# Query parts, weight splits and PSUM banks before the first attention, rearranged

## What is computed

```python
hn = rms_norm(h, kv_norm_g)              # normalised with one gain
v  = hn @ w_v                            # "att_v": units 88 to 95
k  = hn @ w_k                            # "att_kq": even units 96, 98, ...
q  = rms_norm(h, g[0]) @ w_q             # "att_kq": odd units 97, 99, ...
...                                      # scores per head pair, masked softmax, values, then w_o
h = h + rms_norm(m, g[1])
```

## Time and profile before

| what | us |
|---|---|
| median of 3 runs | 2521.54 |
| lowest and highest of them | 2517.85, 2522.76 |
| the profiled execution's own time | 2520.23 |
| its span | 2518.4 |
| TensorE busy in it | 2399.2 |
| VectorE, ScalarE, GpSimd busy | 1370.1, 783.0, 446.5 |

### The profile page before, as it was taken

How to read it: one execution, slowest core, us unless ns; L and a number is a source line. 1 busy time by engine, 2 the same in 40 slices (tenths; PEclk the granted TensorE clock), 3 DMA queues, 4 the chain that set the end, 5 groups by cost and what they waited for, 6 DMA issues and landing times.

```text
span 2518.4 us, 28995 instructions
## 1 busy us (share of the span) xinstructions
PE 2399.2 (95%) x10924; PEld 1934.3 (77%) x10924; DVE 1370.1 (54%) x1951; ACT 783.0 (31%) x1242; POOL 446.5 (18%) x203
## 2 busy tenths in 40 slices
PE   6789999997999899999999999998999999999997
PEld 5677888876766788888788888766877888888886
DVE  5666444446467644434555435789664454444465
ACT  2114323222233333223332223341244343222233
POOL 6670000003545200000000000456540000000000
PEclk8899999997999999999999999999999999999999
DMA  4232433321222233333143332223211343333221
GB/s 169 68 91 67 117 99 94 96 71 50 83 81 84 67 105 96 93 98 102 53 118 100 99 89 81 74 67 93 67 55 55 100 127 91 109 94 99 86 78 54
DMA packets 64833, 221.94 MB, mean 88 GB/s; under 512 B 7504, under 2 KB 9680, under 8 KB 64592
## 3 DMA queue, kind: packets, MB, share of 16 engines
q1 hardware_dynamic: 59184, 208.17, 27.9%
q10 hardware_dynamic: 5536, 12.19, 1.5%
HBM read 218.23 MB, written 2.10 MB: 87 GB/s over the span
## 4 chain that ended last, share of the span: by engine, by line
PE 83%; DVE 11%; ACT 3%; issue 2%; DMA 0%; POOL 0%; ACTq 0%; DVEq 0%; POOLq 0%
PE PS L435 23%; PE PS L437 22%; PE PS L436 22%; PE PS L454 3%; PE PS L531 2%; PE PS L458 1%; DVE SS L1344 1%; DVE MK L1705 1%; PE PS L681 1%; DVE SC L1680 1%; PE PS L505 1%; PE PS L702 1%; PE PS L691 1%; DVE TOP L1704 1%; PE PS L827 1%
## 5 line engine op out<-in xcount | busy, mean ns | idle before, releaser
L435 PE MATMUL PS<-XH,WH 128*128 128x512 f32 x1632 | 647.2, 397 | 19.6 <-DVE T L1542 12.5
L437 PE MATMUL PS<-XH,WL 128*128 128x512 f32 x1632 | 637.0, 390 | 0.0
L436 PE MATMUL PS<-XL,WH 128*128 128x512 f32 x1632 | 636.6, 390 | 0.0
L1332 DVE TENSOR_TENSOR WL<-RAW,WH 128x1024 fp32r<-128x1024 f32 (+3 forms) x308 | 362.2, 1176 | 224.3 <-ACT WH L977 219.7
L378 POOL TENSOR_TENSOR WH<-RAW,ONES 128x1024 fp32r<-128x1024 f32 x91 | 182.7, 2008 | 1437.3 <-DVE WL L1332 735.9
L977 ACT ACTIVATE WH<-RAW 128x1024 fp32r<-128x1024 f32 (+3 forms) x312 | 315.2, 1011 | 354.6 <-DVE M L1449 202.4
L435 PEld LDWEIGHTS PS<-XH,WH 128*128 128x128 f32 x1632 | 307.2, 188 | 101.3 <-issue 22.8
L435 PE MATMUL PS<-HH,WH 128*128 128x512 f32 x928 | 364.1, 392 | 2.6 <-DVE HL L1418 2.6
L437 PE MATMUL PS<-HH,WL 128*128 128x512 f32 x928 | 361.4, 389 | 0.0
L436 PE MATMUL PS<-HL,WH 128*128 128x512 f32 x928 | 361.2, 389 | 0.0
L437 PEld LDWEIGHTS PS<-XH,WL 128*128 128x128 f32 x1632 | 307.1, 188 | 65.1
(11 more groups left out here) (237 smaller groups left out, 2732.8 us busy)
## 6 DMA issues: line engine op xcount, KB each, us to landing
RAW<-in_weights SPq DMA_DIRECT2D x379, 512.0 KB, 3.5
RAW<-in_weights SPq DMA_DIRECT2D x16, 384.0 KB, 3.1
H<-in_xT ACTq DMA_DIRECT2D x8, 256.0 KB, 8.4
BIAS<-in_rel ACTq DMA_DIRECT2D x8, 256.0 KB, 3.5
RAW<-in_weights SPq DMA_DIRECT2D x8, 256.0 KB, 2.6
out<-R ACTq DMA_DIRECT2D x8, 256.0 KB, 2.2
BIAS<-in_rel ACTq DMA_DIRECT2D x8, 224.0 KB, 3.9
DECAY<-in_decay ACTq DMA_DIRECT2D x1, 1024.0 KB, 4.9
```

Source lines behind the costliest of these rows:

```text
L435: nc.tensor.matmul(PS[:, bank_, :], high[:, w], xh[:, k, :], start=(k == 0), stop=False)
L436: nc.tensor.matmul(PS[:, bank_, :], high[:, w], xl[:, k, :], start=False, stop=False)
L437: return nc.tensor.matmul(PS[:, bank_, :], low[:, w], xh[:, k, :], start=False, stop=stop)
L1332: V.tensor_tensor(low[:, 0:w], RAW[:, slot, 0:w], high[:, 0:w].bitcast(F32), ALU.subtract).then_inc(weights_split, 1)
```

## The change

1. `POOL_RANGES` and `WIDE`: units 92 to 99 are no longer split by GpSimd, which goes on at unit 100. Units 92 to 95 move to the slots 4 to 7 and are split by ScalarE and VectorE while units 84 to 87 are taken out. Units 96 to 99 are split by them behind the first half of the values.
2. ScalarE's `pre_norm` and VectorE's `post_and_pre` now make only `XH`/`XL` per tile. The query parts `HH`/`HL` of all eight tiles are made later, behind the first half of the values, two tiles and one weight unit in turn.
3. VectorE no longer waits for the copy `RI` before it takes the first half out of the banks.
4. The second half of the values uses `half_by_banks`, which exists already for another product: six matmuls for one bank, then the next, waiting for one bank at a time.
5. Units 96 and 97 go to banks 6 and 7 (`kq_bank`) and wait for no bank; later ones use 2 and 3 as before.
6. ScalarE issues the loads of `BIAS` only when unit 95 has been multiplied (before: unit 91).

```diff
-POOL_RANGES = ((0, 28), (92, 124), (256, 295))
+POOL_RANGES = ((0, 28), (100, 124), (256, 295))
-WIDE = ((20, 92, 16), (116, 256, 112))
+WIDE = ((20, 96, 16), (116, 256, 112))
...
+        def kq_bank(n):
+            return 2 + n % 2 + (4 if n < FIRST["att_kq"] + 2 else 0)
...
-            products_token_major(xr, stat, lambda k: xp.now() + 2 * k + 1)
+            token_major_half(xr, stat, lambda k: xp.now() + k + 1)
+            spread(5)
+            half_by_banks()
...
                     pe.wait_ge(weights_split, n + 1 + SLOTS)
-                    pe.wait_ge(evacuated, n + 3)
-                last = three_passes(2 + n % 2, n, slice(k * P, k * P + P), xh, xl, k, k == DT - 1)
+                    if n >= kq0 + 2:
+                        pe.wait_ge(evacuated, n + 3)
+                last = three_passes(kq_bank(n), n, slice(k * P, k * P + P), xh, xl, k, k == DT - 1)
...
-            pre_norm([(G_KV, XH), (G_MIX1, HH)], FIRST["att_v"], hn)
+            pre_norm([(G_KV, XH)], FIRST["att_v"], hn)
             norm_rows()
+            act.wait_ge(units_done, FIRST["att_v"] + SLOTS + SLOTS)
+            for t in range(DT):
+                S.activation(HH[:, t, :], H[:, t, :], ACT.Copy, scale=gain(G_MIX1, t)).then_inc(xh_ready, 1)
+                if t % 2 == 1:
+                    split_high(FIRST["att_v"] + DT + t // 2)
...
-            act.wait_ge(units_done, FIRST["att_v"] + SLOTS + SLOTS)
+            act.wait_ge(units_done, FIRST["att_kq"] + SLOTS)
             load_bias(0)
...
-            post_and_pre(G_FFN0_OUT, [(G_KV, XH, XL, x_ready), (G_MIX1, HH, HL, h_ready)])
-            rinv()
+            post_and_pre(G_FFN0_OUT, x_parts(G_KV))
+            recip()
+            sp_.next()
...
             token_major(0, VT)
+            dve.wait_ge(ri_copied, rc.next())
+            for t in range(DT):
+                low_part(t, G_MIX1, HH, HL, h_ready)
+                if t % 2 == 1:
+                    split_low(FIRST["att_v"] + DT + t // 2)
             token_major(1, VT)
```

More of the change, by code:

```diff
@@ L1574, in _ @@
             token_major(0, VT)
+            dve.wait_ge(ri_copied, rc.next())
[3 more added lines that the diff above has]
+                    split_low(FIRST["att_v"] + DT + t // 2)
             token_major(1, VT)
             link(V.memset(BIAS[0:CH, :, SEQ - CH:SEQ], NEG))
+            kq0, out0 = FIRST["att_kq"], FIRST["att_out"]
             def take_k(p):
                 dve.wait_ge(units_done, done.next())
-                V.tensor_tensor(KQ[:, p % 2, :], PS[:, 2, :], RI[:], ALU.mult).then_inc(evacuated, 1)
+                V.tensor_tensor(KQ[:, p % 2, :], PS[:, kq_bank(kq0 + 2 * p), :], RI[:], ALU.mult).then_inc(evacuated, 1)
             def take_q(p):
                 dve.wait_ge(units_done, done.next())
-                V.scalar_tensor_tensor(KQ[:, 2 + p % 2, :], PS[:, 3, :], HD ** -0.5, RI[:], ALU.mult, ALU.mult)\
+                V.scalar_tensor_tensor(KQ[:, 2 + p % 2, :], PS[:, kq_bank(kq0 + 2 * p + 1), :], HD ** -0.5, RI[:], ALU.mult, ALU.mult)\
                  .then_inc(evacuated, 1)
```

## The result

| | before | after |
|---|---|---|
| median of the first comparison | 2519.69 us (4 executions) | 2490.05 us (4 executions) |
| the four executions | 2512.71 to 2522.76 us | 2488.49 to 2492.75 us |
| ratio of the two, 95% interval | | 0.9888 [0.9868, 0.9908] |
| profiled execution: own time, span | 2520.23, 2518.4 us | 2489.05, 2487.2 us |
| first value matmul to first scores | 84.21 us | 61.07 us |

The kernel became faster by 1.1%, 29.6 us between the medians. The changed stage itself came out at 61.07 us where 61.12 us were forecast. The other microseconds lie outside that stage.

What follows compares the result with a forecast made beforehand. TensorE, busy 95% of the span, was taken as the bound. 25.72 + 1.2 + 21.75 + 0 + 12.45 = 61.12 us instead of 84.21 takes 2520.23 to 2497.1; plus 1.3 gives 2498.4 us, range 2494.5 to 2502.5, extended to 2506.

Steps and rivals of the forecast that it cites:

- first half: First value matmul to spread: without GpSimd's splits and the query parts, 25.72 us instead of 40.00, a gain of 14.28 us.
- handover: Spread to second value half: TensorE waits for one eviction instead of copy and four evictions, 1.2 us instead of 4.80.
- second half: Second half of the values: TensorE at the upper clock throughout, 21.75 us instead of 24.71, a gain of 2.96 us.
- wait before the first keys: TensorE's wait for the second half's eviction: 2.25 us goes to 0, since banks 6 and 7 are free.
- keys to scores: First key matmul to first scores: stays as it is, 12.45 us.
- bound of -1.35 us: Start of the first half: the 1.35 us added for a longer lower clock at 570 us might not be needed.
- What would show it: Signs in the profile after: no GpSimd between 565 and 615 us, spread about 596, scores about 631.5, same length behind them.
- last one of the sum: Whole kernel: 23.1 us off the profiled 2520.23 us gives 2497.1, plus 1.3 us to the median gives 2498.4 us.
- VectorE stays the bound: First value half: VectorE's tiles stay at 3.19 us, total gain 19 us, or 8 to 19 with new collisions; chance 0.12.
- The bank order keeps the clock low: Second value half: half clock, 43.5 us instead of 21.75, gain 1.3 us; chance 0.04 with other ways of gaining nothing.
- Query parts too late: Unit 96: TensorE waits for all eight query parts; beyond the 23 us cover attention is delayed, kernel slower; chance 0.02.
- The rule weighed: VectorE and GpSimd share an exclusive SBUF port lock; two-input VectorE operations meeting GpSimd take up to 2.88 us, not 0.75.

Runs made afterwards that it cites:

- before_again: The kernel before, unchanged, profiled and timed once more: 2521.29 us (12 executions), ratio 1.0004 to the same kernel beside it.
- before_g6: The kernel before with GpSimd held back before unit 6 until VectorE's eight squares are done: 2515.55 us, ratio 0.9989.
- only_units: The kernel before with only the split ranges changed (GpSimd leaves out units 92 to 99, `BIAS` loaded later): 2501.29 us, against 2515.97 us beside it.
- no_free_banks: The changed kernel with units 96 and 97 in banks 2 and 3 and their waits as before: 2496.72 us, one execution.
- after_again: The changed kernel, unchanged, profiled and timed once more: 2496.74 us (5 executions), ratio 0.9906.
- after_third: The changed kernel, unchanged, a third time, on one chip beside the kernel before: 2492.03 us (5 executions), ratio 0.9893.
- only_query: The kernel before with only the query parts moved behind the first value half: 2516.46 us, one execution.
- no_by_banks: The changed kernel with the second value half in its old order, waiting for all four banks at once: 2494.43 us, one execution.
- after_g4_again: Repeat of the changed kernel with GpSimd held back before unit 4 until the eight squares are summed: 2487.61 us (4 executions), ratio 0.9874.
- after_g6: The changed kernel with GpSimd held back before unit 6 until the eight squares are summed: 2491.93 us (5 executions), ratio 0.9885.
- after_g4: The changed kernel with GpSimd held back before unit 4 until the eight squares are summed, first run: 2487.89 us (4 executions), ratio 0.9878.

## Why the prediction was wrong

**Right: the stage, step by step.**

| step | forecast | first profile | all three |
|---|---|---|---|
| first half | 25.72 us | 25.72 | 24.24 to 25.72 |
| handover | 1.2 us | 1.17 | 1.16 to 1.17 |
| second half | 21.75 us | 21.85 | 21.84 to 21.88 |
| wait before the first keys | 0 | 0 | 0 |
| keys to scores | 12.45 us | 12.33 | 12.33 |
| stage | 61.12 us | 61.07 | 59.58 to 61.07 |

The bound of -1.35 us for a shorter low clock at the start of the first half was needed: 24.24 us (1.48 below, a little more than the bound) and 24.79 us are such cases. That the first profile agrees to 0.05 us is therefore luck: it happened to have the same six us at the lower clock as the profile that the term was taken from. The base of 84.21 us was also the longest of the three profiles of the old stage (81.11 and 82.30 us in before_again and before_g6), so the stage's gain is 20.0 to 24.6 us by the choice of the pair. What would show it was there too: no GpSimd operation in the stage until unit 96 was multiplied, no VectorE operation on a tile of 128x512 above 0.75 us in the first half, `HL` and `WL` finished by 604.3 us, the clock at 1.00 in the second half, GpSimd's unit 100 at 5.7 us behind the first key matmul. The spread at 596 and the scores at 631.5 us came 4.7 us early, by the start. One sign failed: from the first scores to the end the forecast had the same length, and it was 3.30 us shorter.

**The step that failed** is the last one of the sum: "On the profiled execution's own 2520.23 us this gives 2497.1 us; the median of the runs lies 1.3 us above that execution", with the bound "up to 2.5 us either way by the spread of the runs". It held all that is outside the stage to be fixed, and the median of three runs to be the place of the kernel. The 49 executions of the kernel before that were timed in this study fall in two groups with nothing between 2517.85 and 2519.82 us, each some 6 us wide: 23 with a median of 2516.32 us, and 26 with one of 2521.56 us. The 14 executions of the changed kernel do the same: ten from 2488.49 to 2493.72 us (median 2492.02) and four from 2496.74 to 2497.45 us (median 2497.21). Lower group against lower it is 24.3 us, upper against upper 24.4 us. Two of the three runs that the forecast had were of the upper group, and the four first executions of the changed kernel were all of the lower.

The miss of 8.35 us is then made up of: 2521.54 - 2516.32 = 5.22 us for the group; 24.30 - 23.14 = 1.16 us for a gain larger than forecast; and 2492.02 - 2490.05 = 1.97 us for four executions that lie low in their group. With all 14 executions the median is 2492.4 us and still outside the range, so four lucky executions are not the whole of it: the range was too narrow at its lower end by the group. (Its upper end was not added up rightly either: 1.0 + 1.7 + 2.5 us above the forecast is 2503.6, not 2502.5 us. This played no part.)

**What makes the groups** is shown in part. The start is one cause: of the nine profiled executions without a wait on GpSimd, six had GpSimd's split of unit 6 at 36.66 to 36.91 us and the first value matmul at 569.9 to 571.9 us, and three had it at 37.48 to 37.56 us and the value matmul at 565.5 to 565.7 us. Both kinds are in kernels with the changed stage and with parts of it (early: after, only_units, no_free_banks; late: before, before_again, after_again, after_third, only_query, no_by_banks). The wait of 3.0 us for `SS` is in all six late ones and in no early one. With the race decided by force, the kernel before lost 4.4 us of its median. But after_third started late and ended in the lower group.

A second cause is the stretch from the second attention's last sum (VectorE's copy `AVW`) to its first gate (`GT`). It takes 153.2 us in two profiles (after, no_by_banks), 155.4 to 155.6 in seven (before, only_query, only_units, no_free_banks, after_third, after_g4_again, after_g6) and 158.1 to 158.9 in four (before_again, before_g6, after_again, after_g4). Part of it in after and in after_again:

```profile
1690.00:1721.20 31.20, 25.21 (x104) 20.13 (x102) 29.69 (x69) 3.47 (x5) 20.95 (x11) 0.95 0.38 118
```

```profile
1692.20:1723.40 31.20, 23.71 (x91) 18.48 (x90) 29.72 (x68) 3.56 (x5) 16.19 (x8) 0.84 0.33 101
```

TensorE does 104 matmuls in the one and 91 in the other, at a granted clock of 0.95 and 0.84, with waits in both. Whether the clock causes the longer waits or follows from them, no run separates. A profile with the early start and 153.2 us here was the one that the forecast was measured by; one with the late start and 155.4 us was the one that it was made from. That alone is 4.76 + 2.2 = 7 of the 8 us outside the stage.

**Left open.** Without this stretch, the way from the first scores to the end takes 1708.1 to 1709.7 us in the five profiles that still have both long waits of the stage (before, before_again, before_g6, only_query, only_units), 1709.6 us in no_free_banks, and 1706.4 to 1708.5 us in the seven without them. The difference can be placed but not explained. The attention itself is the same, as forecast: from the first scores to VectorE's next reciprocal `RT` it takes 201.8 us in eleven profiles and 202.3 us in two. From that reciprocal to the third after it, it takes 389.8 to 391.1 us in these five and in no_free_banks, and 388.2 to 389.5 us in the seven. This fits the 1.2 us by which the gain exceeds the forecast. All six of the longer ones have the 2.25 us wait ahead of the first keys; why that should count so much later is not known. Nor was it found what puts TensorE's stretch at the lower clock at 25 to 31 us in one execution and at 31 to 37 us in the next.

**The rivals.** *VectorE stays the bound*: refuted by only_units, where VectorE has even the longer tile and the half takes 26.5 us instead of the 29.7 us by that rival. *The bank order keeps the clock low*: refuted, 1.00 from 592.6 us on. *Query parts too late*: they were done 10 us ahead of the second half's end. **The rule weighed** holds in size once more: 1.78 to 2.88 us for VectorE's operations that meet GpSimd, and at 37 us it can be seen that VectorE's operations, having started first, keep their time, while GpSimd's takes 2.66 instead of 1.89 us.

## What to carry to other kernels

A sum over a stage can be right to 0.1 us and the forecast still miss, when the base it is subtracted from is one of two places where executions fall: before a range is made narrower than the spread of the runs, ask whether the few runs shown are all of one kind, and take that spread whole at both ends. (Here this gives 2498.4 - 1.35 - 4.9 = 2492.2 us as the lower end, which holds the median of all 14 executions, though not that of the first four.) Two engines that stretch each other's operations make a race, and a race is worth deciding: holding GpSimd back for 7 us at the start took another 4.6 us off (2487.8 us over eight executions, against 2492.4 us over 14; 4.4 and 8.9 us on the two chips), more than the order by banks and about as much as the free banks in the execution where the clock fell. Of a change in several parts, one part carried most: taking GpSimd out of the first half gave 10.6 to 13.7 of the 20 to 25 us of the stage.

## What was not expected of the hardware

- A slower TensorE made a faster start. At the lower clock (0.63 us a matmul in the row at 34.09) it released GpSimd 0.86 us later, VectorE's last tile went ahead, and the first eviction came at 45.45 instead of 49.42 us.
- The same wait can cost differently. Behind 2.25 us ahead of the first keys the clock stayed at 1.00 in the kernel before, and it stayed there behind 2.09 us at 598 in no_by_banks. In no_free_banks it was 0.51 for 3.5 us behind the same 2.25 us, and the stretch from first key to first scores took 1.75 us more.
- The changed kernel has a stretch that differs by 5 us from one execution to the next (153.2, 155.4 and 158.3 us in the three profiles of the changed kernel), while three others, each from one reciprocal `RT` of VectorE to the next, take 335.7, 356.8 and 353.1 us (from 225.39, 1218.07 and 2072.57 us in the changed kernel's first profile) and agree within 0.1 us in all thirteen profiles.
